# Moving steps between the queues of a hybrid attention and recurrence layer

## The reference, cut to what matters

```python
h = rmsnorm(x, ln_gain)
z = h @ w_in      # q 1024 | k 256 | v 256 | g_attn 1024 | x_lru 1024 | g_lru 1024
q, k = partial_rope(q), partial_rope(k)        # the first 16 of 64 dims of each head
y_attn = sliding-window attention (window 128, 16 q heads, 4 kv heads, one sink per head)
y_attn = rmsnorm(y_attn * silu(g_attn))
u = causal depthwise conv of width 4 over x_lru
r, i = sigmoid(block-diagonal gates of u);  log_a = -8 r softplus(-lam)
y_lru = linear scan over positions of a, sqrt(1 - a^2) * i * u
y_lru = rmsnorm(y_lru * silu(g_lru))
out = rmsnorm(x + concat([y_attn, y_lru]) @ w_out)
```

## Time and profile before

| | us |
|---|---|
| median of 3 runs | 1403.65 (1402.45 to 1403.94) |
| the profiled execution's own time | 1403.38 |
| its span, first to last instruction | 1401.8 |
| PE busy | 1357.9 |
| DVE busy | 944.4 |
| ACT busy | 811.7 |
| POOL busy | 197.1 |

### The profile page before, as it was taken

One profiled execution on the slowest core, in us unless ns is written; L12 is line 12 of the kernel. 1 busy time (PEld: TensorE's weight loads), 2 busy tenths in 40 slices (PEclk: granted clock), 3 DMA queues, 4 the chain that ended last, 5 costly groups with the idle time before them and its releaser, 6 DMA issues.

```text
span 1401.8 us, 22315 instructions
## 1 busy us (share of the span) xinstructions
PE 1357.9 (97%) x6720; PEld 1104.8 (79%) x6720; DVE 944.4 (67%) x1677; ACT 811.7 (58%) x1679; POOL 197.1 (14%) x251
## 2 busy tenths in 40 slices
PE   4999999999999999999999999999989999999998
PEld 4777777777887888788788888878868888888886
DVE  4787979877776767777676866777676634344342
ACT  5778686948576674848577584857765312212220
POOL 2121202021111202121121202112120000000000
PEclk9999999999999999999999999999999999999999
DMA  8867667573645455463637475454726423233220
GB/s 212 272 227 264 227 226 276 193 259 143 207 150 198 158 206 198 152 220 129 214 135 243 152 258 184 151 189 161 243 77 210 150 60 120 75 105 99 80 90 30
DMA packets 151873, 243.29 MB, mean 174 GB/s; under 512 B 35456, under 2 KB 101248, under 8 KB 151808
## 3 DMA queue, kind: packets, MB, share of 16 engines
q1 hardware_dynamic: 144784, 217.86, 46.2%
q0 software_dynamic: 7024, 24.65, 4.8%
HBM read 179.55 MB, written 62.91 MB: 173 GB/s over the span
## 4 chain that ended last, share of the span: by engine, by line
PE 78%; ACT 8%; DVE 7%; issue 5%; ACTq 1%; DVEq 0%; POOL 0%; POOLq 0%
PE ring L1452 43%; PE acc_b L203 12%; PE ring L203 12%; PE ps_v L1505 3%; PE ps_s L1484 3%; PE ring L1518 2%; ACT p_sb L834 1%; PE ps_t L1492 1%; DVE cu L1279 1%; ACT w_hi L708 1%; ACT ri L900 1%; DVE hs L1322 1%; ACT ra L888 1%; PE ring L1528 1%; PE ring L1464 0%
## 5 line engine op out<-in xcount | busy, mean ns | idle before, releaser
L1452 PE MATMUL ring<-split,w_hi 128*128 128x512 f32 x2304 | 725.0, 396 | 10.6 <-DVE split L1042 5.1
L1452 PEld LDWEIGHTS ring<-split,w_hi 128*128 128x128 f32 x2304 | 425.1, 188 | 107.8 <-issue 12.0
L1452 PE MATMUL ring<-split,w_lo 128*128 128x512 f32 x1152 | 450.4, 391 | 0.0
L1452 PEld LDWEIGHTS ring<-split,w_lo 128*128 128x128 f32 x1152 | 216.8, 188 | 47.3
L633 POOL TENSOR_SCALAR_AFFINE_SELECT p_hi_c<-p_hi 128x512 fp32r<-128x512 f32 x64 | 41.0, 640 | 642.9 <-ACT p_hi L842 642.9
L1279 DVE SCALAR_TENSOR_TENSOR cu<-xl,prm,cu 128x512 f32<-128x512 f32 x96 | 71.9, 749 | 60.4 <-ACT cu L865 57.2
L834 ACT ACTIVATE p_sb<-s_sb,smax 128x129 f32<-128x129 f32 x256 | 99.5, 391 | 0.6
L1729 ACT ACTIVATE w_hi<-res 128x1024 fp32r<-128x1024 f32 x15 | 15.9, 1060 | 134.4 <-DVE res L1799 134.4
L203 PE MATMUL ring<-split,y_own 128*128 128x512 f32 x384 | 91.2, 392 | 0.0
L203 PE MATMUL acc_b<-wo_rest,y_own 128*128 128x512 f32 x384 | 89.7, 390 | 0.0
L203 PEld LDWEIGHTS acc_b<-wo_rest,y_own 128*128 128x128 f32 x384 | 71.9, 188 | 15.3 <-DVE wo_rest L164 0.4
(11 more groups left out here) (209 smaller groups left out, 2349.2 us busy)
## 6 DMA issues: line engine op xcount, KB each, us to landing
w_hi<-w_split_scratch SPq DMA_DIRECT2D x108, 512.0 KB, 3.3
w_lo<-w_split_scratch SPq DMA_DIRECT2D x108, 512.0 KB, 4.2
w_split_scratch<-w_hi SPq DMA_DIRECT2D x36, 512.0 KB, 5.5
w_split_scratch<-w_lo SPq DMA_DIRECT2D x36, 512.0 KB, 6.0
w_raw<-w_in_d SPq DMA_DIRECT2D x32, 512.0 KB, 5.4
y_scratch<-hs POOLq DMA_DIRECT2D x32, 256.0 KB, 4.2
y_scratch<-ya POOLq DMA_DIRECT2D x16, 512.0 KB, 7.2
rows<-y_scratch SPq DMA_DIRECT2D x8, 1024.0 KB, 7.7
```

The lines of the kernel that those rows point to most:

```text
L1452: last = mm(bank(r), w[:, i % WSLOTS, k, :], h[:, par, k, :], start=(k == 0 and j == 0), stop=(k == KC - 1 and j == 2))
```

## The change

x's load is issued at the end of the body before, its square is taken behind high_p(3) of the body before, and the first ones of both stand ahead of the loops. `previous_v` goes from DVE to ACT, and with the high part of v to the end of the body before. On DVE low_p(3) and add_o(2) go ahead of the split of Q1 and of turn_k, and low_gates goes behind conv(0). In `lru_in` the waits are put around the first copy, the carry is read from `xl` and comes last. SP's loads and keeps of the first quarter's last body are interleaved. In the last body high_y(0, 1) goes behind s_exp(3) and gate_l(1), and silu_l(1), lru_tail(1) and low_y(0, 1) go ahead of lru_scan(1). GpSimd's and TensorE's orders are as they were.

```diff
@@ SP, prologue
+            load_x(0, 0)
@@ SP, body
                 load(XL1, COL_XL + P)
-                if q < NQUART - 1:
-                    sp.wait_ge(*ring_ready.at(n, R_XT1 + 1 - NR))
-                    sp.dma_start(xb, x[0, bass.ds((g + (q + 1) * KV) * P, P), :]).then_inc(*x_in.one())
                 sp.wait_ge(*gw_low.at(n, 0))
...
+                if x_follows(q, nxt_par != par):
+                    sp.wait_ge(*ring_ready.at(n, R_XT1 + 1))
+                    load_x(following, q + (nxt_par != par))
@@ ACT
+            def previous_v(n, g):
+                act.wait_ge(*v_kept.at(n, 1))
+                nc.scalar.activation(vraw[:, 0, :], v_carry[:, g, :], ACT.Copy).then_inc(*v_prev.one())
+
             def high_v(n):
+                act.wait_ge(*pv.at(n, NBLK))
                 act.wait_ge(*v_prev.at(n, 1))
+                nc.scalar.activation(v_hl[:, :, 0:HD], vraw[:, :, :], ACT.Copy).then_inc(*v_high.one())
+
+            def high_dv(n):
                 act.wait_ge(*pv.at(n, 0))
-                nc.scalar.activation(v_hl[:, :, 0:HD], vraw[:, :, :], ACT.Copy).then_inc(*v_high.one())
                 act.wait_ge(*dv_raw.at(n, 1))
@@ ACT, prologue
             take_v(-1)
+            previous_v(-1, 0)
+            high_v(-1)
+            square_x(-1)
@@ ACT, lru_in
-                    act.wait_ge(*ring_ready.at(n, r + 1))
                     act.wait_ge(*u_conv.at(n, 3 * u))
-                    act.wait_ge(*i_x.at(n, u + 1 - UNITS))
                     act.wait_ge(*xl_kept.at(n, u))
                     act.sem_inc(settled, 1)
                     nc.scalar.activation(xl[:, 0:CONV - 1], x_carry[:, G, :], ACT.Copy).then_inc(*xl_prev.one())
+                    act.wait_ge(*ring_ready.at(n, r + 1))
+                    act.wait_ge(*i_x.at(n, u + 1 - UNITS))
                     nc.scalar.activation(xl[:, CONV - 1:], bank(r), ACT.Copy).then_inc(*xl_in.one())
-                    act.wait_ge(*xl_prev.at(n, u + 1))
-                    act.sem_inc(settled, 1)
-                    nc.scalar.activation(x_carry[:, G, :], bank(r)[:, T - (CONV - 1):], ACT.Copy
-                                         ).then_inc(*xl_kept.one())
                     act.sem_inc(settled, 1)
                     nc.scalar.activation(cu[u][:, :], bank(r), ACT.Identity, ...
+                    act.wait_ge(*xl_prev.at(n, u + 1))
+                    act.wait_ge(*xl_in.at(n, u + 1))
+                    act.sem_inc(settled, 1)
+                    nc.scalar.activation(x_carry[:, G, :], xl[:, T:], ACT.Copy).then_inc(*xl_kept.one())
@@ ACT, body
-                if q < NQUART - 1:
-                    act.wait_ge(*one_minus.at(n, 0))
-                    square_x(n, x_in.at(n, 1), x_sq, x_norm.at(n, 0))
...
-                high_v(n)
+                high_dv(n)
...
                     act.wait_ge(*ring_ready.at(n, R_GA1 + 1))
-                    proj.high_y(act, 0, 1)
                 s_exp(3)
...
                 gate_l(1)
                 if last:
+                    proj.high_y(act, 0, 1)
...
                 high_p(3)
                 if split_next:
                     split_w(n, NG + XL0)
+                if x_follows(q, nxt_par != par):
+                    square_x(n)
...
                     take_v(n)
+                    previous_v(n, following)
+                    high_v(n)
@@ DVE
-                        if u == 0 and i == 2:
-                            low_gates()
...
                 conv(0)
+                low_gates()
                 low_u(0)
...
-                previous_v(n, g)
                 conv(1)
...
+                if last:
+                    silu_l(1)
                 lru_tail(1)
+                if last:
+                    proj.low_y(dve, 0, 1)
                 lru_scan(1)
                 gate_o(1)
-                silu_l(1)
+                if not last:
+                    silu_l(1)
                 lru_gate(1)
                 if last:
-                    proj.low_y(dve, 0, 1)
                     proj.low_w(dve, 4)
+                low_p(3)
+                add_o(2)
                 if split_next:
                     split_w(n, Q1)
                 if not last:
                     if nxt_par != par:
                         dve.wait_ge(table_in, (q + 2) * 32)
                     turn_k(n, following)
-                low_p(3)
-                add_o(2)
                 gate_o(2)
```

More of the change, by code:

```diff
@@ L366, in phase_a @@
         ring_dve = signal("ring_dve", len(FREED_BY_DVE))
-        x_in = signal("x_in", 1, 16)
-        x_sq = signal("x_sq", 1)
+        x_in = signal("x_in", 1, 16, ahead=1)
+        x_sq = signal("x_sq", 1, ahead=1)
         x_ms = signal("x_ms", 1)
@@ L383, in phase_a @@
         q_low = signal("q_low", 2, ahead=2)
-        v_prev = signal("v_prev", 1)
-        v_high = signal("v_high", 1)
+        v_prev = signal("v_prev", 1, ahead=1)
+        v_high = signal("v_high", 1, ahead=1)
         v_low = signal("v_low", 1)
@@ L453, in bank_free, with x_follows @@
             return ring_dve.at(n, FREED_BY_DVE.index(before) + 1 - late * len(FREED_BY_DVE))
+        def x_follows(q, ends_quarter):
+            return q + ends_quarter < NQUART - 1
         def iterations(eng, body):
@@ L548, in _, with load_x @@
             sp.wait_ge(pro_T, 2 * NBLK)
+            def load_x(g, q):
+                sp.dma_start(xb, x[0, bass.ds((g + (q + 1) * KV) * P, P), :]).then_inc(*x_in.one())
+            load_x(0, 0)
             def body(n, g, par, q, following, nxt_par, split, split_next, last):
@@ L596, in body @@
                     if split:
-                        for i in (GA0, GA1, GL1):
+                        for i in (GA0, GA1):
                             sp.wait_ge(*w_low.at(n, i + 1))
                             keep_group(i, g)
[L601 to L604, removed]
+                        sp.wait_ge(*kept_before(n, KVG))
+                    load_back(n, KVG, following)
+                    if split:
+                        sp.wait_ge(*w_low.at(n, GL1 + 1))
+                        keep_group(GL1, g)
+                        sp.wait_ge(*kept_before(n, Q0))
+                    load_back(n, Q0, following)
+                    if split:
+                        sp.wait_ge(*kept_before(n, Q1))
+                    load_back(n, Q1, following)
                     if q == NQUART - 1 and g == 2:
@@ L709, in split_w, with square_x @@
                                      ).then_inc(*w_high.one())
-            def square_x(n, xin, xsq, free):
-                act.wait_ge(*xin)
-                act.wait_ge(*free)
+            def square_x(n):
+                act.wait_ge(*x_in.at(n, 1))
+                act.wait_ge(*x_norm.at(n, 1))
+                act.wait_ge(*one_minus.at(n, UNITS))
                 nc.scalar.activation(a2[:, :].bitcast(BF16), xb, ACT.Square, accum_out=xs[:, 0:1]
-                                     ).then_inc(*xsq.one())
+                                     ).then_inc(*x_sq.one())
             def root_x(n, xms, xroot):
@@ L910, in decays @@
                     if q < NQUART - 1:
-                        act.wait_ge(*x_sq.at(n, 1))
+                        act.wait_ge(*x_sq.at(n, 0))
                     nc.scalar.activation(a2[:, :], ra[u][:, :], ACT.Square).then_inc(*decay.one())
@@ L925, in body @@
                     split_w(n, GL0)
-                if q < NQUART - 1:
-                    act.wait_ge(*one_minus.at(n, 0))
-                    square_x(n, x_in.at(n, 1), x_sq, x_norm.at(n, 0))
-                elif g == 1:
+                if q == NQUART - 1 and g == 1:
                     proj.high_y(act, 0, 0)
-                elif g > 1:
+                elif q == NQUART - 1 and g > 1:
                     proj.high_w(act, 2 * g - 4)
@@ L1116, in low_q @@
                                         ).then_inc(*q_low.one())
[L1118 to L1122, removed]
             def differ_v(n):
-                dve.wait_ge(*v_prev.at(n, 1))
+                dve.wait_ge(*v_prev.at(n, 0))
                 dve.wait_ge(*ring_act.at(n, FREED_BY_ACT.index(R_VT) + 1 - len(FREED_BY_ACT)))
@@ L1133, in low_v @@
             def low_v(n, g):
-                dve.wait_ge(*v_high.at(n, 1))
+                dve.wait_ge(*v_high.at(n, 0))
                 nc.vector.tensor_tensor(v_hl[:, :, HD:], vraw[:, :, :], f(v_hl[:, :, 0:HD]), ALU.subtract
@@ L1333, in body @@
                 if q < NQUART - 1:
-                    stat_x(x_sq.at(n, 1), x_ms)
+                    stat_x(x_sq.at(n, 0), x_ms)
                 elif g == 1:
```

## The result

The changed kernel takes 1423.26 us (median of 4 runs, 1422.2 to 1424.49), the kernel before 1403.8 beside it (4 runs, 1402.45 to 1404.64). The ratio is 1.014 [1.0122, 1.0157], in brackets its 95% interval: slower by 1.4%, or 19.5 us. The forecast was 1412.5 (1403.0 to 1416.5): right in sign, less than half of the size. The profiled execution is the slowest of the four (1424.49); its span is 1422.9 us, 21.1 more than before.

The account below looks back on a forecast made before the run. PE, busy 97% of the span, was taken to bound the kernel. From 1403.38 us, 16.15 lost at weigh_v(3), 3.6 gained at gates(0) and 3.5 in the last body gave 1412.4, stated as 1412.5; range 1403 to 1416.5.

Parts of the forecast that it names:

- Gates(0) in loop bodies: PE's waits for u_lo ahead of gates(0): 0.6 us gained per body in six loop bodies, 3.6 us.
- Rival 4: Gates(0) doesn't gain since the loop's register steps stay on its path: 3.6 less gained, 1416 us; chance 0.1.
- x's load and square, previous_v, high_v at nothing: These steps, moved to the body's end, cost nothing, as ACT's queue is idle and XL0's parts are needed later.
- The stall of weigh_v(3) in loop bodies: PE stalls for p_lo_c behind the slipped turn_k and sine_k: 1.15 us in each of six bodies, 6.9 us.
- Rival 1: DVE and POOL take no turns beyond those of before, so the slip is 1.6 us: 1404.4 us; chance 0.2.
- Rival 2: POOL's chain doesn't reach PE, so the gains stay, with 1.7 in each of bodies 0 to 2: 1391; chance 0.1.
- Body 3: At weigh_v(3), low_p(3) waits 1.5 us longer for p_hi than turn_k did, against slack 2.57: 1.0 us lost.
- SP's order in body 3 touches no wait of PE: The interleaved loads and keeps on SP's queue in body 3 were taken to change none of PE's waits.
- The last body: Reordered second y: matmuls at 1037.25 instead of 1041.72, weigh_v(3) near 1042.6; gain 3.5 us (bounds 1.8 and 3.9).
- 0 to 2: no slack ... 1.85 + 1.4 + 1.4 = 4.65: In bodies 0 to 2 PE waits for p_lo_c, 2.15 us later, instead of add_o(2): 4.65 us lost net of gains.
- rival 3: In the first quarter XL0's split behind add_k goes ahead of p_lo_c: 1.2 us in each of three bodies, 1416; chance 0.08.

Follow-up runs that it names:

- e7: The kernel before with only lru_in's new order of copies and waits and low_gates behind conv(0): 1397.89 us, 0.9963 of before.
- e1: The changed kernel with POOL's p_current(3), the two selects, ahead of sine_k: 1393.23 us, 0.9926 of the kernel before.
- e2: The changed kernel with low_p(3) and add_o(2) back behind turn_k on DVE: 1395.29 us, 0.9939 of the kernel before.
- e5: The kernel before with only SP's interleaved order of stores and loads in body 3: 1402.09 us, 0.9991 of before.
- e4: The changed kernel with the split of XL0 behind low_k on DVE in bodies 0 to 2: 1418.96 us, 1.0106 of the kernel before.
- e8: e1 with low_p(3) and add_o(2) also ahead of lru_gate(1) and low_w(4) in the last body: 1391.64 us, 0.9916 of the kernel before.
- e9: e8 with DVE's tail as low_p(3), turn_k, add_o(2), gate_o(2), split of Q1: 1392.17 us, 0.9926 of the kernel before.
- e6: The kernel before with only the last body's edits, high_y behind s_exp(3) and low_y ahead of the scan: 1400.72 us, 0.9981 of before.

## Why the prediction was right in sign and short in size

The forecast has 9.05 us lost; the medians lost 19.5, the profiled execution 21.1. Step by step:

- *Gates(0) in loop bodies*, 0.6 each: right. weigh_v(3) starts 0.56 earlier in them on average, and e7, with this edit alone, has them 0.59 shorter and gains 5.0 us, since bodies 1 to 3 gain too, as assumed. Rival 4 (the register steps keep gates(0) late) is out by e7.
- *x's load and square, previous_v, high_v at nothing*: right as far as the runs tell, but it wasn't run alone. Body 11 is 0.3 longer besides its stall, with a wait of 0.23 ahead of KVG for the low part of x (L1068). e1 and e2 have that wait as well, the kernel before and e7 haven't; which moved step makes it is open.
- *The stall of weigh_v(3) in loop bodies*, 1.15: right, 1.19 six times, by the turns named. In 7 and 11 it was 1.04 each, forecast 1.0; in 12 to 14 it was 0.59, forecast 0.54. Rival 1, no turns, is out. Rival 2, POOL's chain not reaching PE, doesn't hold for this change; e1 makes it true by putting the selects ahead of turn_k's work, and is faster by 0.7%, near its 1391.
- *Body 3*: the stall is right (forecast 1.0, measured 1.04), but "SP's order in body 3 touches no wait of PE" is wrong. It takes up to 1.5 off the wait ahead of KVG (e5). The list of waits of the kernel before puts that wait down to "issue", to nothing that it knows. DVE's low part of x had ended at 284.30, the load landed at 285.78, and PE started at 285.87: the landing was the one to read.
- *The last body*: the first wait's end and weigh_v(3)'s start, "near 1042.6", came out to 0.1. The gain over the body is 1.8, not 3.5: the stated lower bound. The reason given with it, that the second wait brings the clock down, is seen in this execution (0.66 behind waits of 0.98 and 2.38) but is only part of it. e4 has the same waits with the clock at 1.00 and gains 2.3. So the clock makes 0.5 of what is lacking; most of the other 1.2 is work that was taken to have moved up as well and hadn't, 0.85 of waiting for wo_rest.
- **The step that failed** is the size of the loss in bodies 0 to 2, "0 to 2: no slack ... 1.85 + 1.4 + 1.4 = 4.65", against 14.6 measured. The mechanism, POOL's selects slipping behind turn_k, was right. Two terms were put at nothing:
  - *The split of XL0 takes a turn ahead of p_lo_c*: 1.14 to 1.17 in each body, 3.4 in all, shown by e4. That was rival 3, at 0.08. In e4, with this turn gone, p_lo_c ends 1.52 or 1.53 later than in the kernel before, 4.6 in all three bodies: the forecast's own 4.65.
  - *The clock*: Q1's projection took 2.6, 1.2 and 2.1 longer, 5.9 in all. The last 0.8 are in weigh_v(3)'s fourth matmul, whose record is 0.79 long instead of 0.50; from its start to the projection's it is 0.6 instead of 0.34. The prediction reckoned with a falling clock in the last body and not here, though it made a longer pause itself: p_lo_c 2.15 later than a place where PE had already waited 1.2. e4, which takes these 1.1 us off the pause and no more, still has 0.51.

The first of these sizes is an experiment's. The second is read from the projection's length at either clock, and in bodies 0 to 2 no run has the pause without the clock's fall. Had this step held both, the sum would have been near 1422.

The Trainium skill's rule in "SBUF — State Buffer", "Who interferes with whom", has issue order decide who blocks. In body 5 this case's order fits it. In body 1 it doesn't, by what the profile shows: the select's record begins at 174.19, the split's at 174.69, and yet the split ran its 1.21 first. The measurement decides; whether the rule's order is one that these records don't show stays open.

## What to carry to other kernels

Work that is moved ahead on one engine moves everything behind it back, and from there what other engines have queued behind that: read the slack of all operands of the next matmuls, not the list of waits, which names only the last one. Here the fix was to move the consumer's inputs out from behind the slipped step in the other engine's queue (e1), worth 30 us. And price a pause of PE of some us by its length and, as a bound, by the matmuls behind it at half clock: here 1.2 to 2.6 us for a projection, 1.6 in the last body, and nothing in e4's last body, behind the same pause. Ask for it at every such pause, and not only where the old trace shows it.

## What was not expected of the hardware

- PE's pauses and the granted clock. It was 0.57 behind waits of 2.68 and 1.67 us (body 1), 0.50 behind 2.69 and 1.68 (body 0) and 0.66 behind 0.98 and 2.38 (last body), over the stretches shown. But it was 1.00 behind 0.97 and 2.41 in e4, as behind 0.98 and 0.60 in e8, and Q1's projection took 8.06, 6.65 and 7.53 behind three pauses that agree to 0.1 us. The length of the pauses alone doesn't settle the clock; what does is open.
- Turns between DVE and POOL. Behind add_k, DVE's split went ahead of a waiting select; behind the multiply, sine_k went ahead of gate_o(2); behind gate_o(2), p_hi_c went ahead of add_k. What decides isn't settled: e4 and e9 each avoided a meeting, and no run told the cases apart. A select that lost ended 0.50 behind the winner's end, in both bodies shown.
- The same load, in kernels with the same order of loads, took 4.70, 4.16 and 4.13 us from issue to landing (KVG's low part in body 3 of the kernel before, e6 and e7), and PE waited for it.
